# Token rows of a mixture of experts fetched as half rows to all 128 partitions, empty places included

## The chip, the cores and the metric

The kernel runs on 1 core of one Trainium2 chip. The time is device microseconds of that core, one launch of the whole kernel. All data are float32.

## The reference, cut to what matters

The kernel computes a hybrid encoder block of 512 tokens by 2048 features: a token mixer (gated DeltaNet heads and sliding-window attention), a layer norm, then a mixture of 32 experts in which every token goes to 2 of them, and a last layer norm. The change lies in the mixture:

```
glog = xt @ w_route_group                       # 4 groups, the best one is taken
elog = xt @ w_route_expert                      # 8 experts in it, the best two are taken
eid, weights = ...                              # 512 tokens x 2
for each expert e (w_gate, w_up: 2048 x 512, w_down: 512 x 2048):
    rows = the tokens that chose e              # 1024 / 32 = 32 in the mean
    hdn = silu(xt[rows] @ w_gate[e]) * (xt[rows] @ w_up[e])
    y[rows] += weight * (hdn @ w_down[e])
out = layer_norm(ALPHA * xt + y)
```

An expert has 12.58 MB of weights, all of them 402.7 MB, and each is read once.

## The kernel before, in words

Up to about 940 us the kernel computes the mixer, with all 512 tokens on the chip. Then come the first norm and the router, and from about 980 us to the end one block of work for each of the 32 experts, in a fixed order ORD, one after another.

The normed rows (not yet with the bias of the norm) are stored to `h1_scr` in HBM, 512 rows of 8 KB. Each expert has 64 places (SLOTS). The router works out on VectorE and TensorE which token lies in which place: `slot_oh` (L1649) says for each token and choice which place it has in its expert, and `slot_table` (L2214) multiplies this by the token's number, less 512, so that column e of a bank holds, on partition s, the token in place s of expert e, and 0 where the place is empty. `idx_tok` (L1665) is that plus 512: a token, or 512 for an empty place. Places are filled from 0 on.

`gather(t)` (L710) is an indirect DMA that GpSimd issues on its own queue: 64 partitions, one row of 8 KB for each. The index 512 of an empty place is beyond the bound, and nothing is fetched for it; the tile was set to zero once, so it holds an old row or zero. The tile `xb` has two halves by partition: an even expert goes to partitions 0 to 63, an odd one to 64 to 127. A gather waits until the rows before it in that half are turned.

`rows_in(t)` (L2256) turns the rows on TensorE, 16 transposes of 64 x 128 into 128 x 64 (L2250), so that the features lie on the partitions; it runs for expert t+1 in the block of expert t, behind the gate and up matmuls. `rows_out` (L1717) adds the bias on VectorE and writes `xbT`. The block (`block_pe`) then has 64 gate and up matmuls (L2274), the turning of the hidden tile (L2267), 32 down matmuls (L2283), and the combination: 16 matmuls (L2243) spread the last expert's 64 rows to the 512 tokens by a one-hot matrix `place`, and VectorE adds each to `r1` (L1706).

The weights come in 12 pieces of 1 MB per expert: 4 of gate, 4 of up, 4 of down, each to all 128 partitions with one run of 8 KB per partition. SyncE issues them in one stream (L637) into a ring of 15 slots (12 from piece 300 on), each as soon as the piece that lay in its slot has been used. Features are dealt to partitions as "(p k)": partition p has features 16p to 16p+15 and a piece takes 4 of them.

The last two experts in the order (ROWS) are no longer combined into the 512 tokens: their rows are summed, normed and stored by themselves. Their residual rows are fetched by one-hot matmuls (`rows_of`, L2295), the 2048 columns lie as two halves of 64 partitions side by side in `rr_row`, the last step (L1840) writes 64 x 512 pieces back to `xb`, four for each expert, and an indirect DMA (L753) stores the 64 rows to `out`.

A second path for experts with over 64 rows (`leftover_...`) is entered only where there are such; it changes along.

Of the kernel before, what the change touches and what calls it, by code (L numbers as in the profile page):

```python
# [30 lines left out]
P = 128  # L31
# [52 lines left out]


def shape_constants():
# [24 lines left out]
    r = np.zeros((P, 3 * E + TT + S), np.float32)  # L111
# [4 lines left out]
    r[:, 3 * E + TT:] = np.arange(S)[None, :]  # L116
    return k, a, r


def build(nc, x, ln0_g, ln0_b, w_in, conv_w, a_log, dt_bias, gdn_norm_w, sinks, w_o, ln1_g, ln1_b,  # L120
# [6 lines left out]
    gate_v = w_gate[0].rearrange("e (p k) f -> p e k f", p=P)  # L127
    up_v = w_up[0].rearrange("e (p k) f -> p e k f", p=P)
# [3 lines left out]
    with ctx:  # L132
# [10 lines left out]
        h1_scr_v = h1_scr.rearrange("(t p) d -> p t d", p=P)  # L143

# [108 lines left out]
        rc = keep("rc", [P, 3 * E + TT])  # L253
# [27 lines left out]
        idx = keep("idx", [P, 2], I32)  # L281
        idx_tok = at("idx_tok", GD + 47 * KB, [P, E], I32)
# [43 lines left out]
        unused = at("unused", MX, [P, 2 * E * CAP // P], I32)  # L326
        ident = cst[:, K_ID:K_ID + P]
# [112 lines left out]
        RT_IDX = RT_W + 3  # L440
# [10 lines left out]
        ROW_DVE = 13  # L451
# [3 lines left out]
        LF_START, LF_TW, LF_ROWS, LF_HID, LF_HI, LF_SPLIT, LF_DVE = 1, 2, 3, 4, 5, 6, 5 + 4 * TT  # L455
# [61 lines left out]

        def lgT_bank(t):
            return [B0, B2][t % 2]
# [12 lines left out]
        def _(sp):  # L532
# [11 lines left out]
            sp.dma_start(rc[:, :], route_consts[:, 0:3 * E + TT]).then_inc(ld_small, 16)  # L544
# [54 lines left out]
            sp.dma_start(tokens[:, :], route_consts[:, 3 * E + TT:]).then_inc(ld_ln1, 16)  # L599
            sp.dma_start(bT[:, :], ln1_b[0].rearrange("(k p) -> p k", p=P), allow_slow_non_contiguous=True).then_inc(ld_ln1, 16)  # L600
            sp.dma_start(b_rows[:, :], ln1_b[0].rearrange("(p k) -> p k", p=P)).then_inc(ld_ln1, 16)
# [4 lines left out]
            def weight_source(e, i):  # L606

                if i < 8:
                    src = [gate_v, up_v][i % 2][:, bass.ds(e, 1), 4 * (i // 2):4 * (i // 2) + 4, :]
                    return src.rearrange("p o k f -> p (o k f)")  # L610
# [40 lines left out]
        def _(pool):  # L651
# [75 lines left out]
            with pool.If(left > 0):  # L727
# [7 lines left out]
                with pool.Fori(0, left) as i:  # L735
                    row = pool.value_load(ovi[0:1, bass.ds(i + LEFTOVER, 1)], min_val=0, max_val=E * CAP - SLOTS)
                    pool.wait_ge(lf_dve, LF_DVE * i + LF_START)
                    for h in range(2):
                        pool.dma_start(idx[SLOTS * h:SLOTS * (h + 1), :], slot_rows[bass.ds(row, SLOTS), :]).then_inc(lf_rows, 16)
                    pool.reg_mov(r_idx, 48 * i + 32)  # L740
                    pool.wait_ge(h1_stored, 16 * TT)
                    pool.wait_ge(lf_rows, r_idx)
                    pool.indirect_dma_start(xb[0:SLOTS, :], None, h1_scr,
                                            bass.IndirectOffsetOnAxis(ap=idx[0:SLOTS, 0:1], axis=0),
                                            bounds_check=S - 1, oob_is_err=False).then_inc(lf_rows, 16)
# [5 lines left out]
            for m in range(LAST):  # L751
                pool.wait_ge(row_dve, ROW_DVE * (m + 1))
                pool.indirect_dma_start(out[0], bass.IndirectOffsetOnAxis(ap=idx_tok[0:SLOTS, ROWS[m]:ROWS[m] + 1], axis=0),  # L753
                                        xb[SLOTS * m:SLOTS * (m + 1), :], None,
                                        bounds_check=S - 1, oob_is_err=False).then_inc(row_stored, 16)
# [3 lines left out]
        def _(act):  # L759
# [319 lines left out]
            def block_act(t):  # L1079
# [16 lines left out]
                for q in range(4):  # L1096
                    j, h = divmod(q, 2)
# [5 lines left out]
            def leftover_act(i):  # L1103
                act.wait_ge(lf_pe, LF_PE * i + LF_XT)
                for g in range(2):
                    a = act.activation(xbT[1][:, 8 * g:8 * g + 8, :], [R0, R1][g][:, :].rearrange("p (k n) -> p k n", k=8), ACT.Copy)
# [7 lines left out]
                for q in range(4):  # L1114
                    j, h = divmod(q, 2)
# [32 lines left out]
            for h in range(2):  # L1148
                rows = slice(SLOTS * h, SLOTS * (h + 1))
                for to, of in ((g2h, g2), (b2h, b2)):  # L1150
                    act.activation(to[rows, :, :], of[rows, :].rearrange("p (j h c) -> p h j c", j=2, h=2)[:, h, :, :],
# [7 lines left out]
        def _(dve):  # L1159
# [469 lines left out]
            for t in range(TT):  # L1629
# [9 lines left out]
            step(dve.tensor_scalar(pos[:, :, 0], rc[:, 3 * E:3 * E + TT], float(-S), None, ALU.add))  # L1639
# [9 lines left out]
            step(dve.tensor_tensor(slot_oh[:, :, :], tokens[:, 0:SLOTS].rearrange("p (o s) -> p o s", o=1).broadcast_to([P, 2 * TT, SLOTS]),  # L1649
                                   pairs(pos[:, :, :], SLOTS), ALU.is_equal))  # L1650
# [14 lines left out]
            step(dve.tensor_scalar(idx_tok[:, :], B2[:, 0:E], float(S), None, ALU.add))  # L1665
            step(dve.tensor_scalar(tok_all[:, :], B2[:, 0:E], float(S), None, ALU.add))
# [7 lines left out]
                                 rc[:, 3 * E:].rearrange("p (t o) -> p t o", o=1).broadcast_to([P, TT, 2])))  # L1674
# [39 lines left out]
            def row_bias(g):  # L1714
                return b_rows[:, 8 * g:8 * g + 8].rearrange("p (k o) -> p k o", o=1).broadcast_to([P, 8, SLOTS])

            def rows_out(t):  # L1717

                for g in range(2):
                    dve.wait_ge(xT_ps, 2 * t + g + 1)  # L1720
                    dve.tensor_tensor(xbT[t % 2][:, 8 * g:8 * g + 8, :], [R0, R1][g][:, :].rearrange("p (k n) -> p k n", k=8),
                                      row_bias(g), ALU.add).then_inc(xT_d, 1)

            def block_dve(t):
# [17 lines left out]
                if t == HOT - 1:  # L1742
                    for m in range(LAST):
                        rows = slice(SLOTS * m, SLOTS * (m + 1))
                        dve.tensor_scalar(one_hot[rows, :], tokens[rows, :], tok_all[rows, ROWS[m]:ROWS[m] + 1], None,
# [7 lines left out]
            def leftover_dve(i):  # L1753
                dve.wait_ge(lf_rows, 48 * i + 48)
                dve.tensor_copy(slot_tw[:, 0:1], idx[:, 0:1])
                dve.tensor_copy(slot_tw[:, 1:2], idx[:, 1:2].bitcast(F32)).then_inc(lf_dve, 1)
                dve.wait_ge(lf_dve, LF_DVE * i + LF_TW)
                dve.tensor_scalar(place[0][:, :], tokens[:, :], slot_tw[:, 0:1], None, ALU.is_equal)
                dve.wait_ge(lf_act, LF_ACT * i + LF_XBT)
                for g in range(2):  # L1760
                    v = xbT[1][:, 8 * g:8 * g + 8, :]
# [60 lines left out]
            def row_norm(m):  # L1822
# [41 lines left out]
        def _(pe):  # L1864
# [381 lines left out]
            def xT(rows, s_):  # L2246

                for g in range(2):
# [3 lines left out]
                    yield i  # L2252

            xbv = xb[:, :].rearrange("s (p k) -> s k p", k=KD)

            def rows_in(t):  # L2256
# [4 lines left out]
                for i in xT(xbv[SLOTS * s_:SLOTS * (s_ + 1), :, :], s_):  # L2261
# [16 lines left out]
            def down(c, w):  # L2278

                for j in range(2):  # L2280
                    for h in range(2):
                        n0 = (2 * j + h) * F
# [4 lines left out]
            def last_down(c, w):  # L2287
                for q in range(4):
                    j, h = divmod(q, 2)
                    i = mm(DN[j][SLOTS * h:SLOTS * (h + 1), :], hidT[:, c, :], w[:, q * F:(q + 1) * F],  # L2290
                           start=c == 0, stop=c == KF - 1)
                    if c == KF - 1:
                        i.then_inc(w_used, 1)

            def rows_of(m, j, t):  # L2295
# [3 lines left out]
                pe.wait_ge(comb_done, 4 * TT * (t - 1) + (8 if j == 0 else 16))  # L2299
                for tt in range(TT):  # L2300
                    for h in range(2):
                        i = mm(R1[SLOTS * h:SLOTS * (h + 1), :], slot_hot[:, tt, SLOTS * m:SLOTS * (m + 1)],
                               r1[:, tt, (2 * j + h) * F:(2 * j + h + 1) * F], start=tt == 0, stop=tt == TT - 1)
# [55 lines left out]
            def leftover_pe(i):  # L2359
                pe.wait_ge(lf_rows, 48 * i + 48)  # L2360
                for k in range(KD):
                    a = mm([R0, R1][k // 8][:, (k % 8) * SLOTS:(k % 8 + 1) * SLOTS], xbv[0:SLOTS, k, :],
                           cst[0:SLOTS, 0:SLOTS], start=True, stop=True)
# [53 lines left out]
```

## Time and profile before

| | us |
|---|---|
| median of 3 runs | 2006.78 (2005.09 to 2007.88) |
| the profiled execution's own time | 2011.87 |
| its span, first to last instruction | 2010.3 |
| TensorE busy | 1864.9 (93%) |
| VectorE busy | 1031.2 (51%) |
| ScalarE busy | 632.4 (31%) |
| GpSimd busy | 356.6 (18%) |
| mean granted TensorE clock | 0.972 |

The span is a few us shorter than the time of the execution. In the page's 40 slices the share of the 16 DMA engines is 2 to 4 tenths in most slices up to about 900 us and 9 tenths or more in every slice from about 1000 us to 1960 us, where they move some 400 GB/s. A high busy share of an engine says that it had something to do, not that the end waited for it: the chain of waits and the rows of waiting say that.

### The profile page before, as it was taken

To read this page: it belongs to the slowest core of one execution; us is meant where nothing else is said; L and a number is where in the kernel's file an instruction comes from. 1 tells how busy PE (TensorE), PEld (TensorE's weight loads), DVE (VectorE), ACT (ScalarE), POOL (GpSimd) and SP (SyncE) were. 2 spreads that over 40 slices of the span, in tenths; PEclk is the share of its full clock that TensorE was granted. 3 is DMA by queue.
4 is the path that set the end of the run, shared out by engine and by line. 5 is a ranking of instruction groups with operands and counts; after the bars stand their busy time and mean duration, and the time that the engine had idled before them with its cause. 6 is when DMAs were issued, how large, how long until landed. Compare 5 with 4: busy or idle time off the path is not lost.

```text
span 2010.3 us, 25805 instructions
## 1 busy us (share of the span) xinstructions
PE 1864.9 (93%) x10588; PEld 1132.9 (56%) x10588; DVE 1031.2 (51%) x1732; ACT 632.4 (31%) x1040; POOL 356.6 (18%) x292
## 2 busy tenths in 40 slices
PE   5999999999999998999799898998989898988996
PEld 4777887788778777888433333433333333333332
DVE  6456665666533554334655444535444454544356
ACT  6323332243234554113233223231322323132323
POOL 0343333343234322542100000000000000000000
PEclk9999999999999999999799999999999999999998
DMA  7223212222223214438699999999999999999995
GB/s 258 77 64 85 64 51 68 73 64 63 64 72 84 64 53 178 137 105 307 239 400 397 396 405 393 414 398 403 404 400 413 402 413 404 407 402 409 405 400 223
DMA packets 171014, 505.48 MB, mean 251 GB/s; under 512 B 18480, under 2 KB 108720, under 8 KB 117328
## 3 DMA queue, kind: packets, MB, share of 16 engines
q1 hardware_dynamic: 167552, 490.56, 64.3%
q0 software_dynamic: 2768, 9.05, 1.7%
q10 hardware_dynamic: 576, 4.19, 0.5%
q8 instruction: 86, 1.41, 0.3%
q14 instruction: 32, 0.26, 0.0%
HBM read 498.92 MB, written 13.76 MB: 255 GB/s over the span
## 4 chain that ended last, share of the span: by engine, by line
PE 56%; DMA 30%; DVE 9%; ACT 2%; issue 2%; SPq 1%; POOL 0%; DVEq 0%; POOLq 0%; ACTq 0%
DMA ring<-in_w_up 29%; PE bank L2274 10%; PE bank L1869 10%; PE bank L1871 9%; PE bank L1870 9%; PE bank L2283 3%; PE bank L2243 2%; DVE half L1266 1%; PE bank L2016 1%; PE bank L2007 1%; DVE att L1472 1%; DVE sc L1467 1%; PE bank L2025 1%; SPq L637 1%; DVE sc L1487 1%
## 5 line engine op out<-in xcount | busy, mean ns | idle before, releaser
L2274 PE MATMUL bank<-ring,xbT 128*64 128x512 f32 x2048 | 488.7, 621 | 76.0 <-DMA ring<-in_w_up 72.6
L667 POOL TENSOR_TENSOR wlo<-raw,whi 128x512 fp32r<-128x512 f32 x232 | 312.3, 1377 | 525.5 <-ACT whi L790 370.5
L1706 DVE TENSOR_TENSOR r<-r,bank 128x512 f32<-128x512 f32 x464 | 287.7, 682 | 219.5 <-PE bank L2243 219.5
L2274 PEld LDWEIGHTS bank<-ring,xbT 128*64 128x64 f32 x2048 | 155.5, 142 | 362.6 <-issue 359.2
L1869 PE MATMUL bank<-hTh,wlo 128*128 128x512 f32 x704 | 299.8, 426 | 1.9 <-DVE hTl L1199 1.2
L1871 PE MATMUL bank<-hTh,whi 128*128 128x512 f32 x704 | 276.4, 393 | 0.0
L1870 PE MATMUL bank<-hTl,whi 128*128 128x512 f32 x704 | 276.4, 393 | 0.0
L2283 PE MATMUL bank<-ring,hidT 128*64 128x512 f32 x992 | 219.5, 595 | 0.5 <-ACT hidT L1084 0.5
L1711 DVE TENSOR_TENSOR yhl<-yw,yhl 64x512 fp32r<-64x512 f32 x120 | 82.7, 690 | 227.8 <-ACT yhl L1101 224.9
L714 POOL DMA_INDIRECT xb<-h_scr,idx_tok x32 | 31.3, 978 | 899.3 <-PE bank L2250 878.6
L790 ACT ACTIVATE whi<-raw 128x2048 fp32r<-128x2048 f32 x50 | 95.6, 1913 | 199.0 <-PE bank L1871 199.0
L1099 ACT ACTIVATE yw<-bank,wts_all 64x512 f32<-64x512 f32 x120 | 81.6, 680 | 226.7 <-PE bank L2283 224.4
L1869 PEld LDWEIGHTS bank<-hTh,wlo 128*128 128x128 f32 x704 | 132.8, 189 | 32.1 <-issue 3.3
L1871 PEld LDWEIGHTS bank<-hTh,whi 128*128 128x128 f32 x704 | 132.4, 188 | 29.9
L1082 ACT ACTIVATE hid<-bank 64x512 f32<-64x512 f32 x32 | 18.8, 588 | 410.0 <-PE bank L2274 410.0
L2283 PEld LDWEIGHTS bank<-ring,hidT 128*64 128x64 f32 x992 | 69.5, 137 | 135.7 <-issue 135.1
L1870 PEld LDWEIGHTS bank<-hTl,whi 128*128 128x128 f32 x704 | 133.2, 189 | 19.3 <-issue 0.2
L2243 PE MATMUL bank<-yhl,place 128*128 128x512 f32 x480 | 143.8, 421 | 0.0
L2243 PEld LDWEIGHTS bank<-yhl,place 128*128 128x128 f32 x480 | 80.8, 188 | 86.6 <-issue 73.9
L1869 PE MATMUL bank<-whi,mxl 128*128 128x512 f32 x256 | 99.7, 389 | 0.7 <-ACT mixT L969 0.7
L1871 PE MATMUL bank<-whi,mxh 128*128 128x512 f32 x256 | 99.6, 389 | 0.0
L1870 PE MATMUL bank<-wlo,mxh 128*128 128x512 f32 x256 | 99.6, 389 | 0.0
(371 smaller groups left out, 2066.9 us busy)
## 6 DMA issues: line engine op xcount, KB each, us to landing
ring<-in_w_gate SPq DMA_DIRECT2D x128, 1024.0 KB, 28.4
ring<-in_w_up SPq DMA_DIRECT2D x128, 1024.0 KB, 29.1
ring<-in_w_down SPq DMA_DIRECT2D x128, 1024.0 KB, 27.8
raw<-in_w_in SPq DMA_DIRECT2D x44, 1024.0 KB, 5.7
raw<-in_w_o SPq DMA_DIRECT2D x16, 1024.0 KB, 5.0
xt<-in_x SPq DMA_DIRECT2D x4, 1024.0 KB, 8.9
h_scr<-xt SPq DMA_DIRECT2D x4, 1024.0 KB, 7.9
r<-h_scr SPq DMA_DIRECT2D x1, 4096.0 KB, 12.5
```

Source lines behind the costliest of these rows:

```text
L667: i = pool.tensor_tensor(wlo[sl][:, part, :], raw[sl][:, :].rearrange("p (k n) -> p k n", k=KD)[:, part, :], whi[sl][:, part, :].bitcast(F ...
L714: pool.indirect_dma_start(xb[half_, :], None, h1_scr, bass.IndirectOffsetOnAxis(ap=idx_tok[0:SLOTS, ORD[t]:ORD[t] + 1], axis=0), bounds_ch ...
L790: act.activation(whi[sl][:, :, :].rearrange("p k n -> p (k n)"), raw[sl][:, :], ACT.Copy).then_inc(strip_hi, 1)
L1099: act.activation(yw[lo_, q, :], rows, ACT.Copy, scale=wts_all[lo_, ORD[t]:ORD[t] + 1])
L1706: dve.tensor_tensor(v, v, comb_bank(q, tt)[:, :], ALU.add).then_inc(comb_done, 1)
L1711: dve.tensor_tensor(yhl[SLOTS:P, q, :], yw[SLOTS:P, q, :], yhl[SLOTS:P, q, :].bitcast(F32), ALU.subtract).then_inc(yw_split, 1)
L1869: mm(bank, lo_, rh, start=first, stop=False)
L1870: mm(bank, hi_, rl, start=False, stop=False)
L1871: return mm(bank, hi_, rh, start=False, stop=final)
L2243: mm(comb_bank(q, tt)[:, :], place[n % 2][:, tt * P:(tt + 1) * P], yhl[:, q, :], start=True, stop=True).then_inc(comb_ps, 1)
L2274: i = mm(GU[SLOTS * h:SLOTS * (h + 1), :], xT_[:, k, :], w[:, kk * F:(kk + 1) * F], start=k == 0, stop=k == KD - 1)
L2283: i = mm(DN[j][SLOTS * h:SLOTS * (h + 1), :], hidT[:, c, :], w[:, n0:n0 + F], start=c == 0, stop=c == KF - 1)
```

## The change

Everything goes by half rows. `h1_scr` and `out` are seen as 1024 half rows of 4 KB, half row 2n+h being half h of token n. The partition q of a gather fetches half q // 64 of the token in place q % 64, so one gather fills 128 partitions x 1024 columns, and `xb` has its two buffers side by side in the columns. Index of a filled place: 2 x token + half. Index of an empty place: q itself, so that partition q fetches half row q of the scratch; nothing is beyond the bound any more.

The places are dealt to the partitions in another order (place b*8+a to partition a*8+b, in both halves). The features are dealt as "(h p k)": each half has its own 8 per partition, for the weights of gate and up, the bias and the turned rows. Turning takes 8 transposes of 128 x 128 instead of 16. The column quarters that go to each down bank are swapped so that a bank holds column quarters j and j+2. The rows of the last two experts need no moving back: two 128 x 512 steps instead of four of 64 x 512, and their store is one of half rows, where empty places are beyond the bound and skipped, as before. One small VectorE operation is added in the router ahead of the first gather, and one for each of the last two experts.

```diff
-    gate_v = w_gate[0].rearrange("e (p k) f -> p e k f", p=P)
+    gate_v = w_gate[0].rearrange("e (h p k) f -> p e h k f", h=2, p=P)
+    r[:, R_HALF:R_HALF + 1] = i // SLOTS
+    r[:, R_OWN:R_OWN + 1] = i
+    r[:, R_TO_OWN:R_TO_OWN + 1] = 2 * S + i // SLOTS - i
+        h1_halves = h1_scr.rearrange("s (h d) -> (s h) d", h=2)
+        out_halves = out[0].rearrange("s (h d) -> (s h) d", h=2)
+        xb_half = [xb[:, i * D // 2:(i + 1) * D // 2] for i in range(2)]
...
             def gather(t):
-                half_ = slice(SLOTS * (t % 2), SLOTS * (t % 2 + 1))
                 if t >= 2:
                     pool.wait_ge(xT_ps, 2 * (t - 1))
-                pool.indirect_dma_start(xb[half_, :], None, h1_scr,
-                                        bass.IndirectOffsetOnAxis(ap=idx_tok[0:SLOTS, ORD[t]:ORD[t] + 1], axis=0),
-                                        bounds_check=S - 1, oob_is_err=False).then_inc(gathered[t % 2], 16)
+                pool.indirect_dma_start(xb_half[t % 2], None, h1_halves,
+                                        bass.IndirectOffsetOnAxis(ap=idx_tok[:, ORD[t]:ORD[t] + 1], axis=0),
+                                        bounds_check=2 * S - 1, oob_is_err=False).then_inc(gathered[t % 2], 16)
...
-            step(dve.tensor_tensor(slot_oh[:, :, :], tokens[:, 0:SLOTS].rearrange("p (o s) -> p o s", o=1).broadcast_to([P, 2 * TT, SLOTS]),
-                                   pairs(pos[:, :, :], SLOTS), ALU.is_equal))
+            step(dve.tensor_tensor(slot_oh[:, :, :].rearrange("p j (a b) -> p j a b", a=8),
+                                   tokens[:, 0:SLOTS].rearrange("p (o b a) -> p o a b", o=1, b=8).broadcast_to([P, 2 * TT, 8, 8]),
+                                   ...
-            step(dve.tensor_scalar(idx_tok[:, :], B2[:, 0:E], float(S), None, ALU.add))
-            step(dve.tensor_scalar(tok_all[:, :], B2[:, 0:E], float(S), None, ALU.add))
+            step(dve.tensor_scalar(tok_all[:, :], B2[:, 0:E], 0.0, rc[:, R_TO_OWN:R_TO_OWN + 1], ALU.is_lt, ALU.mult))
+            step(dve.scalar_tensor_tensor(out=idx_tok[:, :], in0=tok_all[:, :], scalar=rc[:, R_OWN:R_OWN + 1], in1=B2[:, 0:E],
+                                          op0=ALU.add, op1=ALU.add))
+            step(dve.tensor_scalar(tok_all[:, :], B2[:, 0:E], 0.5, float(S), ALU.mult, ALU.add))
...
                 for j in range(2):
-                    for h in range(2):
-                        rows = slice(SLOTS * h, SLOTS * (h + 1))
-                        dve.scalar_tensor_tensor(out=xb[SLOTS * m:SLOTS * (m + 1), (2 * j + h) * F:(2 * j + h + 1) * F],
-                                                 in0=rr_row[m][j][rows, :], scalar=nm_r[rows, m, 3:4], in1=b2h[rows, j, :],
-                                                 op0=ALU.mult, op1=ALU.add).then_inc(row_dve, 1)
+                    dve.scalar_tensor_tensor(out=xb_half[m][:, j * F:(j + 1) * F], in0=rr_row[m][j][:, :], scalar=nm_r[:, m, 3:4],
+                                             in1=b2h[:, j, :], op0=ALU.mult, op1=ALU.add).then_inc(row_dve, 1)
...
             for m in range(LAST):
                 pool.wait_ge(row_dve, ROW_DVE * (m + 1))
-                pool.indirect_dma_start(out[0], bass.IndirectOffsetOnAxis(ap=idx_tok[0:SLOTS, ROWS[m]:ROWS[m] + 1], axis=0),
-                                        xb[SLOTS * m:SLOTS * (m + 1), :], None,
+                pool.indirect_dma_start(out_halves, bass.IndirectOffsetOnAxis(ap=idx_last[:, m:m + 1], axis=0),
+                                        xb_half[m], None,
...
                 for g in range(2):
-                    for k in range(8):
-                        i = pe.transpose([R0, R1][g][:, k * SLOTS:(k + 1) * SLOTS], rows[:, 8 * g + k, :],
-                                         cst[SLOTS * s_:SLOTS * (s_ + 1), K_ID + SLOTS * s_:K_ID + SLOTS * (s_ + 1)])
+                    for k in range(4):
+                        i = pe.transpose([R0, R1][g][:, k * P:(k + 1) * P], xbv[s_][:, 4 * g + k, :], ident)
```

## Rows read from the trace of the kernel before

**Rows 1.** The page's DMA queues: packets, MB, share of 16 engines.
```profile
q1 hardware_dynamic: 167552, 490.56, 64.3%
q0 software_dynamic: 2768, 9.05, 1.7%
```
**Rows 2.** Busy time of the engines by stretch: PE, PEld, DVE, ACT, POOL, PEclk, DMA share, GB/s.
```profile
1112.60:1890.50 777.90, 702.99 (x3205) 288.34 (x3204) 361.21 (x584) 211.10 (x339) 22.15 (x24) 0.97 1.01 404
```
**Rows 3.** What PE waited for, 1100 to 1940 us: total, times, longest.
```profile
PE bank L2274 <- DMA ring<-in_w_up: 72.6, 60, 4.6
```
**Rows 4.** The chain of waits, 1700 to 1910 us: start, us, what.
```profile
1800.66 31.48 DMA ring<-in_w_up
1832.13 0.14 issue
1832.27 6.47 PE bank L2274 x16
...
1887.86 1.90 PE bank L2250 x16
```
**Rows 5.** GpSimd in order of time: gathers of experts 4, 5, 7 and 31.
```profile
1029.47 0.92 POOL L714 DMA_INDIRECT xb<-h_scr,idx_tok  x1 [26.36 <-PE bank L2250]
1057.07 0.92 POOL L714 DMA_INDIRECT xb<-h_scr,idx_tok  x1 [26.68 <-PE bank L2250]
...
1112.62 0.92 POOL L714 DMA_INDIRECT xb<-h_scr,idx_tok  x1 [26.72 <-PE bank L2250]
...
1890.53 0.92 POOL L714 DMA_INDIRECT xb<-h_scr,idx_tok  x1 [34.07 <-PE bank L2250]
```
**Rows 6.** The DMA view, 1320 to 1340 us, a stretch without a gather.
```profile
DMA packets 1156, 8.42 MB, mean 421 GB/s; under 512 B 129, under 2 KB 129, under 8 KB 129
```
**Rows 7.** The DMA view by queue, 1112.6 to 1890.5 us, 24 gathers.
```profile
q1 hardware_dynamic: 42225, 307.51, 98.1%
q0 software_dynamic: 1920, 6.41, 3.0%
```
**Rows 8.** The same, 14 us from the gather of expert 14, 1340.0 to 1354.0 us.
```profile
q1 hardware_dynamic: 720, 5.24, 93.9%
q0 software_dynamic: 80, 0.29, 7.2%
```
**Rows 9.** The same for expert 15, 1369.8 to 1383.8 us.
```profile
q1 hardware_dynamic: 636, 4.63, 90.8%
q0 software_dynamic: 80, 0.39, 10.5%
```
**Rows 10.** The same for expert 23, 1625.9 to 1639.9 us.
```profile
q1 hardware_dynamic: 735, 5.36, 99.1%
q0 software_dynamic: 80, 0.08, 2.4%
```
**Rows 11.** DMA issues: KB each, median us to landing.
```profile
ring<-in_w_gate SPq DMA_DIRECT2D x128, 1024.0 KB, 28.4
ring<-in_w_down SPq DMA_DIRECT2D x128, 1024.0 KB, 27.8
raw<-in_w_in SPq DMA_DIRECT2D x44, 1024.0 KB, 5.7
raw<-in_w_o SPq DMA_DIRECT2D x16, 1024.0 KB, 5.0
out<-r SPq DMA_DIRECT2D x4, 1024.0 KB, 4.8
```
**Rows 12.** Groups by form, 940 to 2011 us: busy us, mean ns, idle before.
```profile
L2190 PE MATMUL bank<-cst,r 128*128 128x128 f32 x64 | 7.8, 275 | 0.0
L1831 DVE SCALAR_TENSOR_TENSOR rr_row<-rr_row,nm_r,g2h 128x512 f32<-128x512 f32 x4 | 2.8, 747 | 0.2
L1665 DVE TENSOR_SCALAR idx_tok<-bank 128x32 int32<-128x32 f32 x1 | 0.2, 192 | 0.2 <-PE bank L2218 0.2
```
**Rows 13.** All engines in order of time, the first transposes and the end.
```profile
949.65 1.97 PE L2190 MATMUL bank<-cst,r 128*128 128x128 f32 x16
...
1956.01 0.69 DVE L1734 TENSOR_TENSOR hid<-hid,bank 64x512 f32<-64x512 f32 x1 [1.68 <-ACT hid L1082]
...
2001.46 3.09 DVE L1840 SCALAR_TENSOR_TENSOR xb<-rr_row,nm_r,b2h 64x512 f32<-64x512 f32 x4
2005.36 0.92 POOL L753 DMA_INDIRECT out<-xb,idx_tok  x1 [12.26 <-DVE xb L1840]
```

More of the change, by code:

```diff
@@ L83 @@
 J_END = J_SLOPE + QH
+R_HALF = 3 * E + TT
+R_ROW = R_HALF + 1
+R_OWN = R_ROW + 1
+R_TO_OWN = R_OWN + 1
+R_END = R_TO_OWN + 1
 def shape_constants():
@@ L281, in build @@
         idx = keep("idx", [P, 2], I32)
+        idx_half = keep("idx_half", [P, 1], I32)
+        idx_last = keep("idx_last", [P, LAST], I32)
         idx_tok = at("idx_tok", GD + 47 * KB, [P, E], I32)
@@ L516, in ps64, with turned_rows, by_halves @@
             return b[rows, 0:TT * H].rearrange("p (c i) -> p c i", c=TT)
+        def turned_rows(b):
+            return b[:, :].rearrange("p (k h n) -> p k h n", k=4, h=2)
+        def by_halves(tile, g):
+            return tile[:, :, :].rearrange("p (h k) n -> p k h n", h=2)[:, 4 * g:4 * g + 4, :, :]
         def lgT_bank(t):
@@ L598, in _ @@
             sp.dma_start(b1[:, :], ln1_b[0].partition_broadcast(P)).then_inc(ld_ln1, 16)
[L599 removed]
+            sp.dma_start(tokens[:, :], route_consts[:, R_END:]).then_inc(ld_ln1, 16)
             sp.dma_start(bT[:, :], ln1_b[0].rearrange("(k p) -> p k", p=P), allow_slow_non_contiguous=True).then_inc(ld_ln1, 16)
[L601 removed]
+            sp.dma_start(b_rows[:, :].rearrange("p (h k) -> p h k", h=2), ln1_b[0].rearrange("(h p k) -> p h k", h=2, p=P)).then_inc(ld_ln1, 16)
             sp.dma_start(wr[:, :, 0:GROUPS], w_route_group[0].rearrange("(k p) n -> p k n", p=P)).then_inc(ld_ln1, 16)
@@ L1105, in leftover_act @@
                 for g in range(2):
-                    a = act.activation(xbT[1][:, 8 * g:8 * g + 8, :], [R0, R1][g][:, :].rearrange("p (k n) -> p k n", k=8), ACT.Copy)
+                    for h in range(2):
+                        a = act.activation(by_halves(xbT[1], g)[:, :, h, :], turned_rows([R0, R1][g])[:, :, h, :], ACT.Copy)
                 a.then_inc(lf_act, 1)
@@ L1150, in _ @@
                 for to, of in ((g2h, g2), (b2h, b2)):
-                    act.activation(to[rows, :, :], of[rows, :].rearrange("p (j h c) -> p h j c", j=2, h=2)[:, h, :, :],
+                    act.activation(to[rows, :, :], of[rows, :].rearrange("p (h j c) -> p h j c", j=2, h=2)[:, h, :, :],
                                    ACT.Copy).then_inc(rows_act, 1)
@@ L1638, in _ @@
                                    top[:, :, 0:1].rearrange("p t o -> p (t o)"), ALU.subtract))
-            step(dve.tensor_scalar(pos[:, :, 0], rc[:, 3 * E:3 * E + TT], float(-S), None, ALU.add))
+            step(dve.tensor_scalar(pos[:, :, 0], rc[:, 3 * E:3 * E + TT], float(-S), 2.0, ALU.add, ALU.mult))
             assert k_[0] == RT_M
@@ L1720, in rows_out @@
                     dve.wait_ge(xT_ps, 2 * t + g + 1)
-                    dve.tensor_tensor(xbT[t % 2][:, 8 * g:8 * g + 8, :], [R0, R1][g][:, :].rearrange("p (k n) -> p k n", k=8),
-                                      row_bias(g), ALU.add).then_inc(xT_d, 1)
+                    dve.tensor_tensor(by_halves(xbT[t % 2], g), turned_rows([R0, R1][g]), row_bias(g), ALU.add).then_inc(xT_d, 1)
             def block_dve(t):
@@ L1744, in block_dve @@
                         rows = slice(SLOTS * m, SLOTS * (m + 1))
+                        dve.tensor_scalar(idx_last[:, m:m + 1], tok_all[:, ROWS[m]:ROWS[m] + 1], 2.0, rc[:, R_HALF:R_HALF + 1],
+                                          ALU.mult, ALU.add)
                         dve.tensor_scalar(one_hot[rows, :], tokens[rows, :], tok_all[rows, ROWS[m]:ROWS[m] + 1], None,
@@ L1760, in leftover_dve @@
                 for g in range(2):
-                    v = xbT[1][:, 8 * g:8 * g + 8, :]
+                    v = by_halves(xbT[1], g)
                     a = dve.tensor_tensor(v, v, row_bias(g), ALU.add)
@@ L2244, in combine @@
                        start=True, stop=True).then_inc(comb_ps, 1)
-            def xT(rows, s_):
-                for g in range(2):
-                    for k in range(8):
-                        i = pe.transpose([R0, R1][g][:, k * SLOTS:(k + 1) * SLOTS], rows[:, 8 * g + k, :],
-                                         cst[SLOTS * s_:SLOTS * (s_ + 1), K_ID + SLOTS * s_:K_ID + SLOTS * (s_ + 1)])
-                    yield i
-            xbv = xb[:, :].rearrange("s (p k) -> s k p", k=KD)
+            xbv = [xb_half[i].rearrange("s (p k) -> s k p", k=KD // 2) for i in range(2)]
             def rows_in(t):
@@ L2260, in rows_in @@
                     pe.wait_ge(comb_done, 16 * (t - 2) + 10)
-                for i in xT(xbv[SLOTS * s_:SLOTS * (s_ + 1), :, :], s_):
+                for g in range(2):
+                    for k in range(4):
+                        i = pe.transpose([R0, R1][g][:, k * P:(k + 1) * P], xbv[s_][:, 4 * g + k, :], ident)
                     i.then_inc(xT_ps, 1)
@@ L2287, in last_down @@
             def last_down(c, w):
[L2288 to L2293, printed above, removed]
+                for j in range(2):
+                    for h in range(2):
+                        n0 = (2 * h + j) * F
+                        i = mm(DN[j][SLOTS * h:SLOTS * (h + 1), :], hidT[:, c, :], w[:, n0:n0 + F],
+                               start=c == 0, stop=c == KF - 1)
+                        if c == KF - 1:
+                            i.then_inc(w_used, 1)
             def rows_of(m, j, t):
@@ L2360, in leftover_pe @@
                 pe.wait_ge(lf_rows, 48 * i + 48)
-                for k in range(KD):
-                    a = mm([R0, R1][k // 8][:, (k % 8) * SLOTS:(k % 8 + 1) * SLOTS], xbv[0:SLOTS, k, :],
-                           cst[0:SLOTS, 0:SLOTS], start=True, stop=True)
+                for k in range(KD // 2):
+                    a = mm([R0, R1][k // 4][:, (k % 4) * P:(k % 4 + 1) * P], xbv[0][:, k, :], ident, start=True, stop=True)
                 a.then_inc(lf_pe, 1)
```

54 lines of the change are left out of this document (30 added, 24 removed).

## The prediction

> **What bounds the kernel now.** I read the page's slices, then the stretch of the expert blocks, then who waits for whom, then the chain, and last the DMA view stretch by stretch. TensorE is the busiest engine of the page, but in the blocks it is busy 703 of 778 us, while the DMA engines stand at 1.01 of their time and move 404 GB/s [rows 2]. Between 1100 and 1940 us TensorE waits 60 times, 72.6 us in all, and all of it is for weights [rows 3]. So the weight stream sets the pace there. The first blocks, which still live on pieces that were loaded ahead, take 27.6 us each (1057.07 less 1029.47); the 24 from expert 7 to 31 take (1890.53 - 1112.62) / 24 = 32.4 us [rows 5]. The chain says until when: its last piece of waiting for weights ends at 1832 us, and from there it runs through TensorE and VectorE to the end [rows 4]. What shortens the weight stream before 1832 us comes out of the total; what shortens TensorE counts only after.
>
> The stream has a rate of its own: 421 GB/s where no gather runs [rows 6]. Over the 24 gathers that would be 777.9 x 0.421 = 327.5 MB on the weights' queue q1, and it moved 307.5 [rows 7]. So a gather with what comes along displaces (327.5 - 307.5) / 24 = 0.83 MB of weights, though it fetches only 6.41 / 24 = 0.27 MB. Instruction fetches and the like are a few hundredths of that, so I take 0.81 MB, or 0.81 / 0.421 = 1.93 us of the stream for each gather. By its bytes it would be 0.63 us. The excess is what the change can win or lose.
>
> **How one gather's price comes about.** 14 us at 421 GB/s are 5.89 MB. Expert 23 fetches 0.08 MB, some 10 rows, and displaces 5.89 - 5.36 = 0.53 MB [rows 10]. Expert 14 fetches 0.29 MB, 35 rows, and displaces 0.65 [rows 8]. Expert 15 fetches 0.39 MB, 48 rows, and displaces 1.26 [rows 9]. So the price is not one per byte: it has a floor near 0.5 to 0.65 MB that 10 rows reach as 35 do, and about doubles beyond. I read that as skew. 64 partitions over 16 engines are 4 places each; places are filled from 0 on, so 10 rows already give one engine its full 4, and the stream, in which each piece needs all 16 engines, goes by the slowest. 4 rows x 8 KB on one engine are 32.8 KB; at 421 / 16 = 26.3 GB/s that is 1.25 us, or 0.52 MB of the whole stream, and the cheap gathers show 0.53 and 0.65. Beyond 32 places a second set of engines writes too, and the price goes to twice that, as if two engines shared one way into the same partitions.
>
> The Trainium skill has a rule for such a sharing ("SBUF — State Buffer", section "Door 1: The DMA port swizzle"): partition p and p+32 lie on the same DMA port, and 64 partitions reach only half of the ports. By it a gather with over 32 rows puts up to 8 rows on one port, 2.5 us or 1.05 MB, and one with fewer puts 4, 1.25 us; the rows above for experts 14, 15 and 23 agree roughly. By it alone the new gather would cost 1.25 us always.
>
> **The change part by part.**
>
> *The gathers.* Now every engine gets 8 half rows of 4 KB, 32.8 KB, whatever the number of tokens. Bytes go from 0.27 to 0.52 MB a gather, while the largest load of one engine stays at 32.8 KB. The rows go to all 128 partitions as the weights do, so the doubling beyond 32 rows goes. What no row shows is the price c of one 4 KB packet of this queue in an engine's time; a gather costs 8c. Below: at the stream's rate 4.1 KB / 26.3 GB/s = 0.156 us, a gather 1.25 us. Above: an 8 KB row on the slowest engine now costs at most 0.65 / 0.421 / 4 = 0.39 us [rows 8]; if a packet has that price whatever its size, a gather costs 3.1 us. Packet size matters little in this trace: 1 MB in runs of 512 B lands in 5.7 us (w_in), in runs of 2 KB in 5.0 (w_o), in runs of 8 KB in 4.8 (out) [rows 11]. So I take a value near the lower end, half of 0.39 and a little: c = 0.20 us, 1.6 us a gather. Against 1.93 us that is 0.33 us won. The gathers that count are those in the full stream: from expert 2 on, and up to the last that the chain still waits behind, some 26 (experts 2 to 27; the last wait for weights comes earlier when the stream is faster). 26 x 0.33 = 8.6 us off. The break-even is c = 1.93 / 8 = 0.24 us. The ends are 26 x (1.25 - 1.93) = -17.7 us and 26 x (3.1 - 1.93) = +30 us.
>
> *The weights' new order.* A piece still has runs of 8 KB per partition, but they lie 16 KB apart instead of 32 KB. Gate has 32 KB now and down has 8 KB, and they land in 28.4 and 27.8 us [rows 11], so a distance between 8 and 32 KB makes no difference that is clear. I take 0. If all of 28.4 against 27.8 came from the distance, half the way back would gain some 1% of the stream, and at the other end I leave a loss as large, 1% or 8 us; that lies inside the range.
>
> *Turning the rows.* 16 transposes take 1.90 us on the chain [rows 4]. The form with 128 partitions is in the trace at 1.97 us for 16 [rows 13] and 275 ns each, as pipelined [rows 12]; 8 take 0.99 us, so 0.9 us of TensorE per block goes. Up to 1832 us the weights hide that: worth nothing. After it, four or so such places are on TensorE; but the next step waits for ScalarE's and VectorE's hidden tile, 1.3 us behind the gate and up matmuls (0.60 and 0.69 us), so at most 1.90 - 1.3 = 0.6 us is won, and none where the chain goes by VectorE's xbT and sums. I take 0.8 us in all; between 0 and 2.4. If TensorE's cover were gone everywhere it would be worth more, never less. VectorE's writing of xbT in the new order has as many elements; 0.
>
> *The router.* One more VectorE operation of 0.19 us, with its gap 0.21 us [rows 12], ahead of the first gather and of everything that VectorE does behind it, which is on the path to the first block: +0.2 us. slot_oh has as many elements in another order; 0, at most doubled, +0.7 us. The first gather is no later than that: its rows are turned well ahead of the last router step.
>
> *The end.* Of the last expert's four 64 x 512 steps, 3.09 us [rows 13], two of 128 x 512 remain; the form is at 747 ns each [rows 12], so 1.5 us goes, all of it on the chain. The store behind has 128 half rows, skips the empty ones and has no more bytes. It can land up to half a us sooner if the rows are spread better, and GpSimd's issue (0.92 us) could grow with 128 indices: I take -0.2, between -0.6 and +1. The two small operations for idx_last run in the blocks that wait for weights: 0. Extra constants and smaller pieces of the bias land long before their use: 0.
>
> Sum: -8.6 - 0.8 + 0.2 - 1.5 - 0.2 = -10.9 us. On the profiled execution, 2011.87 us, that is 2001.0; its time lies 5.1 us over the median of the runs, so from the median it is 2006.8 - 10.9 = 1996.
>
> **The rivals.**
>
> *The dips stay and the bytes are added (slower).* The excess is then no skew but the price of mixing two queues of any load: a gather keeps its 1.93 - 0.63 = 1.30 us and pays for 0.52 MB instead of 0.27, 1.24 us: 2.54 us. 27 x 0.61 = +16.5 us, less 2.5 for the end and TensorE: 2021 us. It decides from c = 0.24 us on. For it: the stream is full all the time, so 8.2 MB more must go somewhere; packets of both queues are slow in the dip. Against it: 0.08 MB and 0.29 MB have nearly the same price, 0.39 MB twice that, which no fixed excess gives. The Trainium skill's page "DMA: Bandwidth & Descriptors" (section on the anatomy of a DMA) has a DMA cost a constant plus its bytes, which speaks for this rival; by that formula 0.26 MB more at 436 GB/s are an estimated 0.6 us a gather, 16 us in all.
>
> *No net change in the stream.* The fine packets and the doubled bytes eat just what the spreading gives, c between 0.22 and 0.26. Then the end and TensorE remain: 2004 us, 2000 to 2009. For it: the break-even lies in the middle of the range that the rows leave.
>
> *Wholly by the slowest engine (faster still).* c = 0.156: 26 x 0.68 = 17.7 us, and 2.3 beside: 1987 us. This is the far end of the forecast rather than another mechanism.
>
> *TensorE becomes the bound.* Its blocks need 27.6 us against 32.4 now and 32.1 forecast [rows 5], so only the blocks with extra row work near the end come to it, which the count of 26 already holds. No chance of its own.
>
> **How the numbers follow.** Forecast, with its far end, 0.66: 1985 to 2001, centre 1996. No net change 0.15. Bytes added 0.19: 2009 to 2025, centre 2021. Under 0.2%, 4 us, a measurement of this kernel can't tell from no change. Faster by over that (below 2002.8): 0.66 and a little of the second, 0.68. Within: 0.12. Slower: 0.20. The range must reach into the slower case until 1 in 10 is left above: 1985 to 2015. The likeliest case's own is 1987 to 2001.
>
> **What would show it.** Right: in the 14 us behind a gather the weights' queue moves about 5.2 MB whatever the expert, with 0.52 MB on q0; the even pace replaces the 4.6 to 5.4 of now; blocks take 32.1 us; q0's bytes of the whole rise by about 8 MB from 9.05 [rows 1], q1's stay; the mean of the DMA stage rises towards 410 GB/s; the last VectorE steps are two of 0.75 us. Wrong: q1 at 4.8 MB behind every gather (bytes added), or dips as deep for few tokens as for many but longer than 1.6 us; a rate below 421 GB/s between the gathers would convict the weights' new order; a chain in which a wait for xb stands would convict the gather's landing.

## The result, and the profile after

| | before | changed |
|---|---|---|
| median of the runs, us | 2006.35 (4 runs) | 1987.19 (1981.77 to 1990.13, 4 runs) |
| profiled execution's own time | 2011.87 | 1989.5 |
| its span | 2010.3 | 1987.9 |
| TensorE busy | 1864.9 | 1843.3 (93%) |

The ratio is 0.9893, with a 95% interval of 0.9877 to 0.9909: 1.1% or 21 us faster; the two medians lie 19.2 us apart. The forecast was 1996 us, 10.9 us faster. The direction and the place were right, the size was half of what came.

What TensorE waited for between 1100 and 1940 us in the changed kernel (total, times, longest), beside [rows 3]:

```profile
PE bank L2295 <- DMA ring<-in_w_up: 62.3, 67, 4.1
PE bank L2288 <- DVE hid L1761: 8.7, 27, 0.3
```

Its chain of waits around the last wait for weights, beside [rows 4] (start, us, what):

```profile
1755.53 26.89 DMA ring<-in_w_up
1782.41 0.14 issue
1782.55 0.04 PE bank L2295
1782.59 30.92 DMA ring<-in_w_up
1813.51 0.14 issue
1813.64 5.33 PE bank L2295 x16
```

The kernel still lives on the weight stream, now until 1813.5 us instead of 1832.1: 18.6 us of the 22.4 are gained ahead of this point. In the profiled execution the mixer ended 3.1 us later than in that of before (the clearing of `xb` starts at 962.16 against 959.08 us). I take that for scatter: in the profiles of the other kernels below, all with the same mixer, it starts anywhere from 957.0 to 961.7 us. Counted from there, the stream gained 21.7 us.

The DMA view of the changed kernel over the gathers of experts 7 to 29, 1114.59 to 1797.98 us (GB/s in 40 slices; then by queue packets, MB, share of 16 engines):

```profile
GB/s 421 419 422 420 421 420 422 420 421 421 420 421 418 423 419 421 420 421 421 421 421 419 421 420 421 421 422 420 421 420 421 422 420 421 419 421 421 421 421 421
q1 hardware_dynamic: 37828, 275.46, 96.9%
q0 software_dynamic: 3168, 11.54, 4.2%
```

The same for the kernel before, its own experts 7 to 29, 1112.62 to 1816.89 us:

```profile
GB/s 375 422 395 382 416 382 422 378 422 400 420 375 422 402 395 397 397 421 395 421 391 422 393 420 398 391 419 398 421 397 420 405 414 396 388 421 377 420 404 419
q1 hardware_dynamic: 38157, 277.91, 98.0%
q0 software_dynamic: 1760, 6.02, 3.2%
```

This is the finding in two rows. Before, 23 of the 40 slices lie between 375 and 405 GB/s; after, none is below 418, though the gathers move twice the bytes (11.54 MB against 6.02). What a gather displaces, by the working of the prediction over these 22: before 704.27 x 0.421 - 277.91 = 18.6 MB, 0.84 MB each or 2.0 us; after 683.39 x 0.421 - 275.46 = 12.2 MB, 0.56 MB each or 1.3 us. It moves 0.52 MB, so almost nothing is left beside its bytes. The blocks take 31.06 us ((1797.98 - 1114.59) / 22) against 32.01. Over experts 7 to 31, the stretch that the forecast used, they take (1871.26 - 1114.59) / 24 = 31.5 us, against 32.1 forecast and 32.4 before.

The 14 us behind the gather of expert 15 in the changed kernel, 1359.46 to 1373.46 us, beside [rows 9]:

```profile
q1 hardware_dynamic: 732, 5.34, 91.9%
q0 software_dynamic: 144, 0.52, 9.4%
```

The dearest gather of before displaced 1.26 MB, this one 5.89 - 5.34 = 0.55. The same view gives the time of one half row in an engine: 9.4% of 16 engines x 14 us are 21.1 us, over 128 half rows 0.165 us each (the other 16 packets of q0 are small).

The end of the changed kernel (VectorE's last step, now two of 128 x 512, and the store), beside [rows 13]:

```profile
1980.71 1.42 DVE L1868 SCALAR_TENSOR_TENSOR xb<-rr_row,nm_r,b2h 128x512 f32<-128x512 f32 x2
1982.93 1.00 POOL L775 DMA_INDIRECT out<-xb,idx_last  x1 [9.65 <-DVE xb L1868]
```

### The profile page after: what moved, and what is told of

Its sections match the earlier page's. It is cut to its first block, busy times and chain, and to the rows that moved or that the text cites. A ratio compares the mean times of both kernels' runs of the same rounds, so it can differ in the third digit from the quotient of the medians.

```text
span 1987.9 us, 25292 instructions
## 1 busy us (share of the span) xinstructions
PE 1843.3 (93%) x10332; PEld 1113.7 (56%) x10332; DVE 1028.5 (52%) x1731; ACT 632.7 (32%) x1040; POOL 358.9 (18%) x292
## 3 DMA queue, kind: packets, MB, share of 16 engines
q8 instruction: 84, 1.38, 0.3%
## 4 chain that ended last, share of the span: by engine, by line
PE 54%; DMA 32%; DVE 9%; ACT 2%; issue 2%; POOL 0%; SPq 0%; POOLq 0%; DVEq 0%; ACTq 0%
DMA ring<-in_w_up 32%; PE bank L1896 10%; PE bank L2295 9%; PE bank L1897 9%; PE bank L1898 9%; PE bank L2304 3%; PE bank L2270 2%; DVE half L1289 2%; PE bank L2043 1%; PE bank L2034 1%; DVE att L1495 1%; DVE sc L1490 1%; PE bank L2052 1%; DVE sc L1510 1%; PE bank L2324 1%
## 5 line engine op out<-in xcount | busy, mean ns | idle before, releaser
L2295 PE MATMUL bank<-ring,xbT 128*64 128x512 f32 x2048 | 479.7, 611 | 65.3 <-DMA ring<-in_w_up 62.3
```

Of the source, the lines that this page charges most:

```text
L2295: i = mm(GU[SLOTS * h:SLOTS * (h + 1), :], xT_[:, k, :], w[:, kk * F:(kk + 1) * F], start=k == 0, stop=k == KD - 1)
```

## The experiments

Each ratio is to the kernel before on the same chip, in brackets its 95% interval.

**What is undone first: the fetching of empty places**, in three orders of the places. All three keep the half rows and the 128 partitions.

```diff
+            step(dve.tensor_scalar(idx_tok[:, :], B2[:, 0:E], rc[:, R_ROW:R_ROW + 1], None, ALU.add))   # empty: 2 * S + half
```

> The changed kernel with one thing undone: an empty place has an index beyond the bound again and fetches nothing. Places lie as in the change (place b*8+a on partition a*8+b). Bytes of a gather fall from 0.52 to 0.27 MB. Bytes theory (a gather over 128 partitions costs what it moves, in any order): 0.63 us a gather instead of 1.27, 27 gathers, 17 us off the changed kernel's 1987: 1970, 0.982 of before. Slowest-engine theory with an engine for 8 neighbouring partitions: each engine has 4 filled of 8, also 1970. Slowest-engine theory with an engine for partitions p to p+3 and p+32 to p+35 (p a multiple of 4): the filled places of an expert with 32 rows all lie on every other engine, 8 half rows each, so the price stays 1.25 us: 1987, 0.990. Skipping theory (the skipped places themselves made the dips before): the dips come back, 1.9 us a gather: 2004, 0.999.

Measured: 1984.3 us, 0.9892 [0.9876, 0.9909].

The natural order of the places, `tokens[:, 0:SLOTS]` again in `slot_oh`:

> The changed kernel with empty places skipped and the places in their natural order, place s on partitions s and s+64. Bytes theory: 1970, 0.982. Engine for 8 neighbouring partitions: 32 rows fill 8 half rows on half of the engines, 1.25 us as now: 1987, 0.990. Engine for p to p+3 and p+32 to p+35: up to 32 rows give 4 half rows to each engine, 0.62 us, and more than 32 give 8 to some, 1.25 us; about half of the experts each: 0.94 us in the mean, 9 us off: 1978, 0.986. Skipping theory: 2004.

Measured: 1974.2 us, 0.985 [0.983, 0.9871].

The places spread, from a table of constants:

```diff
+    r[:, R_SLOT:R_SLOT + SLOTS] = (8 * (4 * (q // 32) + q % 4) + q % 32 // 4)[None, :]
```

> The changed kernel with empty places skipped and place s put on partition 32*(s//32) + 4*(s%8) + (s//8)%4 of each half, so that consecutive places go to different groups of partitions. Engine for p to p+3 and p+32 to p+35: n rows give each engine n/8 half rows rounded up, 4.2 in the mean, 0.65 us: 27 x 0.62 = 17 us off the changed kernel: 1970, 0.982, the best of the three. Engine for 8 neighbouring partitions: 32 rows fill partitions 0 to 31 of each half, 1.25 us: 1987. Bytes theory: 1970. Skipping theory: 2004.

Measured: 1968.9 us, 0.9818 [0.9802, 0.9835]. The same bytes in three orders give three times, so bytes are not all (the intervals of the second and the third just touch; a later run of the third gave 0.9816 again). Skipping as such costs nothing, which fells that theory. The order of the three, and their sizes, are those of the slowest engine with an engine for partitions p to p+3 and p+32 to p+35 (expected 1987, 1978, 1970). The Trainium skill ("DMA: Bandwidth & Descriptors", section "The descriptor swizzle") states this assignment for a transfer to 128 partitions; the three times agree with it, and the rival with 8 neighbouring partitions would have put the first at 1970 and the third at 1987.

The traces of the first and the third over experts 7 to 29 (1113.71 to 1793.80 us, and 1113.34 to 1781.65 us) say how the slowest engine acts:

```profile
GB/s 419 419 424 418 423 418 421 422 420 420 420 422 420 421 419 422 419 421 420 422 420 419 414 419 417 415 410 420 418 414 422 419 416 403 417 416 410 392 423 421
DMA packets 41324, 284.11 MB, mean 418 GB/s; under 512 B 5934, under 2 KB 5934, under 8 KB 7402
q1 hardware_dynamic: 38125, 277.65, 98.6%
```
```profile
DMA packets 40887, 280.93 MB, mean 420 GB/s; under 512 B 5886, under 2 KB 5886, under 8 KB 7354
q1 hardware_dynamic: 37688, 274.47, 98.8%
```

With places on every other engine the 22 blocks take 680.1 us, spread 668.3 us, and yet the rates are 418 and 420 GB/s, which explains 3 us of the 12. In the slower one 3.2 MB more had arrived in the stretch for the same 22 blocks. I read that as the lightly loaded engines running ahead into pieces that are not complete; that was not measured engine by engine. The slices fit it: up to the middle they stand at 418 to 424 GB/s, gathers or not, and later some fall, to 392 at the lowest. One such fall is at 1747 to 1749 us, 15 us behind the gather of expert 27, when that gather has long landed: 324 GB/s. So uneven load makes no dip at its gather. It adds up over the experts and comes out later.

**Whole rows, nothing skipped.** The kernel before, with an index of its own for each empty place:

```diff
+    r[:, R_OWN:R_OWN + 1] = i % SLOTS
+    r[:, R_TO_OWN:R_TO_OWN + 1] = S - i % SLOTS
...
```

> The kernel before with one thing changed: an empty place fetches a whole row of its own (row number = place), so 64 rows of 8 KB go to 64 partitions every time, 0.52 MB, as many bytes as in the change. Theory of the shared way into the partitions (64 partitions are reached by half of the ways): 8 rows on each way, 65.5 KB, 2.5 us a gather against 1.93 before: 27 x 0.57 = 15 us slower, 2021, 1.008. Slowest engine alone, no shared way: 4 rows on each of 16 engines, 1.25 us, 18 us faster: 1988, 0.991. Skipping theory: the dips go with the skipping, 1988 too. Bytes on top of a fixed excess: 2.54 us, 2022.

Measured: 2042.5 us, 1.0188 [1.0168, 1.0209]. 14 us behind the gather of expert 15, 1381.7 to 1395.7 us:

```profile
GB/s 398 398 421 445 421 375 421 492 398 398 421 445 398 187 187 211 211 281 234 187 234 281 234 304 234 304 421 421 421 421 445 398 375 445 445 445 398 445 445 375
q1 hardware_dynamic: 620, 4.51, 85.7%
q0 software_dynamic: 80, 0.52, 15.3%
```

The direction is that of the shared way, and just as well that of bytes on top of a fixed excess (2022); this run can't tell them apart. The size is over both: 5.89 - 4.51 = 1.38 MB or 3.3 us, where 2.5 were expected by both and 1.3 is what the same bytes cost in the change. For 4.5 us (13 slices of 0.35) the two queues together run at little over half of their rate, so the weights alone at less than that. So neither the number of bytes (the change moves as many) nor the skipping makes the dip, but something about whole rows to 64 partitions: the size of the row, or the 64.

**Half rows in two gathers of 64 partitions.**

```diff
-                pool.indirect_dma_start(xb_half[t % 2], None, h1_halves, ... idx_tok[:, ...]
+                for h, ix in enumerate((idx_tok, idx_hi)):
+                    pool.indirect_dma_start(xb_half[t % 2][SLOTS * h:SLOTS * (h + 1), :], None, h1_halves, ... ix[0:SLOTS, ...]
```

> The changed kernel with one thing changed: each gather is issued as two, the first half rows to partitions 0 to 63, then the second to 64 to 127. The same 128 half rows of 4 KB, the same bytes, the same place order, nothing skipped. Two small operations of VectorE more in the router (+0.4 us). Shared-way theory (64 partitions are reached by half of the ways, all 16 engines crowd on them): the dips come back, at the price that whole rows to 64 partitions with nothing skipped had for the same bytes, 3.1 us against 1.3: 27 x 1.8 = 48 us slower than the changed kernel, 2035, 1.014 of before. By bytes and the load of each engine alone: nothing changes but a second issue: 1988, 0.990.

Measured: 2039.5 us, 1.0165 [1.0141, 1.0189]. 14 us behind the gathers of expert 15, 1377.67 to 1391.67 us:

```profile
GB/s 398 515 445 375 375 421 421 421 398 445 468 351 410 246 257 304 199 351 199 316 293 211 363 222 293 269 257 316 258 386 375 445 398 398 445 375 421 421 468 468
q1 hardware_dynamic: 617, 4.51, 88.5%
q0 software_dynamic: 160, 0.52, 13.4%
```

The dip is back with 4 KB rows, so it is not the size of the row. What is left is the 64 partitions of a DMA, or that there are two DMAs for each expert; the whole rows above had a dip with one.

**Two gathers of 128, each filling 64.** Who writes, or where to? The same partitions are filled one half after the other, but by DMAs that span all 128.

```diff
+                    if h:
+                        pool.wait_ge(gathered[t % 2], 32 * (t // 2) + 16)
+                    pool.indirect_dma_start(xb_half[t % 2], None, h1_halves, ... ix[:, ...]     # the other half's indices are beyond the bound
```

> The changed kernel with each gather issued as two over all 128 partitions: the first has its indices for partitions 64 to 127 beyond the bound and fills 0 to 63, the second the reverse, and waits for the first. The same bytes go to the same partitions as in the kernel with two gathers of 64 partitions; what differs is the shape of the DMA and so which engine writes which partition. If the dips come of engines that write to partitions that are another engine's in the weights' DMAs (the deal of 64 rows to 16 engines): no dips, 1.3 us for both, 1989, 0.991. If they come of 64 partitions being reached at a time, whoever writes them: as with two gathers of 64, 2035, 1.016. If the slowest engine sets the price with no leeway (8 engines have 8 half rows, then the other 8): 2 x 1.25 us, 33 us over the changed kernel: 2020, 1.006.

Measured: 1992.2 us, 0.9927 [0.9911, 0.9942]. The 20 us that hold both gathers of expert 16, 1394.4 to 1414.4 us:

```profile
GB/s 475 393 393 475 410 426 393 442 410 377 426 385 434 434 369 451 434 377 475 377 459 410 393 459 377 459 410 426 402 402 418 402 451 410 377 467 442 393 442 377
q1 hardware_dynamic: 1073, 7.82, 94.0%
q0 software_dynamic: 288, 0.52, 7.1%
```

No dip, 47 us less than with gathers of 64, for the same bytes to the same partitions. The dips hang on the DMA's shape. The second gather waits for the first here, which the kernel with gathers of 64 did not do; but the changed kernel sends all 128 half rows at once and has no dip either. The reading that fits is the expected one: in a DMA to 64 partitions some engines write to partitions that belong to others in the weights' DMAs. That is argued and not shown: which engine writes what in such a DMA is seen in no view here.

**Whole rows, places spread over blocks of four.**

```diff
+    r[:, R_SLOT:R_SLOT + SLOTS] = (16 * (q % 4) + q // 4)[None, :]
```

> The kernel before with places put on its 64 partitions in another order, place s on partition 4*(s%16) + s//16, so that 32 rows give two to each block of four partitions; skipping and bytes as before. If a DMA to 64 partitions gives each of 16 engines four neighbouring partitions, and the slowest engine sets the price: 2.2 rows in the mean, 0.7 us instead of 2.0: 35 us faster than before, 1970. If the shared way sets it, 8 ways get n/8 rows each, 4.3 in the mean, 1.35 us: 1988, 0.991. If the price goes with the bytes as in the kernel with whole rows and nothing skipped (1.28 MB for 0.52), 0.67 MB for 0.27, 1.6 us: 1995, 0.994. If it is something else about 64 partitions, no change, 2005.

Measured: 2018.4 us, 1.0056 [1.0038, 1.0075], slower, which no theory had. Expert 15 (0.39 MB, 47 or 48 rows), 1374.9 us on, and expert 23 (10 rows), 1632.31 us on, 14 us each:

```profile
q1 hardware_dynamic: 673, 4.89, 91.6%
...
q1 hardware_dynamic: 769, 5.60, 99.4%
```

Displaced are 1.00 and 0.29 MB, in place of 1.26 and 0.53 [rows 9, 10]: for these two cheaper. Yet over experts 7 to 29 (1114.54 to 1823.90 us) it is 0.92 MB a gather against 0.84, so others got dearer. So the floor that 10 rows had depends on where the rows lie, but spreading them over more of the 64 partitions wins nothing in the mean. Why it costs more is not shown; that more rows then lie in another engine's partitions is a guess.

**The weights' order alone**, on the kernel before:

```diff
-    gate_v = w_gate[0].rearrange("e (p k) f -> p e k f", p=P)
+    gate_v = w_gate[0].rearrange("e (h p k) f -> p e h k f", h=2, p=P)
...
```

> The kernel before with the change's order of the features alone: gate and up weights and the bias dealt as (h p k), the columns of the rows picked to match; whole rows, 64 partitions, 16 transposes, skipping as before. Expected by every theory: 0, 2005 (within 4 us), 421 GB/s between gathers. If runs 16 KB apart instead of 32 KB were read better, part of the change's gain is here: 1 to 1% faster.

Measured: 2006.9 us, 0.9991 [0.998, 1.0002]. Nothing, as forecast.

**What all gathers still cost.** This kernel leaves out the gathers of experts 2 to 31:

```diff
+                if t < 2:
                     pool.indirect_dma_start(xb_half[t % 2], None, h1_halves,
...
```

> The changed kernel without the gathers of experts 2 to 31: their blocks compute on the rows of experts 0 and 1 (the output leaves the others' rows out). This measures what all gathers still cost. 1.27 us x 27 = 34 us off the changed kernel: 1953, 0.974, unless TensorE's own 27.6 us a block, or its longer blocks near the end, come to bound first; the stream alone needs 12.58 / 0.421 = 29.9 us a block, so they should not before the last six.

Measured: 1950.8 us, 0.9719 [0.9701, 0.9736]: 33 to 36 us under the medians of the changed kernel (1984.0 and 1987.2), where 27 gathers at 1.27 us had given 34. The gathers that are left cost their bytes, and leaving them out gives that back.

**One shared half row for all empty places:**

> The changed kernel with one thing changed: every empty place fetches the same half row (half 0 or 1 of token 0) instead of one of its own; 32 reads in the mean of the same 4 KB in each half. By bytes and engines: 1987, 0.990. If reads of one place in HBM wait for each other, and since every engine has 4 of them in the mean: dearer; at twice the time for these packets 27 x 0.6 = 17 us, 2004, 0.999.

Measured: 1982.9 us, 0.9887 [0.9872, 0.9902], against 0.9899 of the changed kernel on the same chip: no difference. A place of its own for each empty one buys nothing.

**The change and the best version side by side:**

> The changed kernel itself, beside the others of this call: 1987, 0.990 of before.

> Empty places skipped and places spread over the groups of partitions, once more and in more rounds, beside the changed kernel on the same chip. By the traces a gather displaces 0.31 MB instead of 0.56: 27 x 0.25 / 0.421 = 16 us faster than the changed kernel: 1970, 0.982 of before.

Measured: 1984.0 us, 0.9899 [0.9884, 0.9915], and 1968.7 us, 0.9816 [0.98, 0.9832]. Skipping with spread places beats both kernels, by 0.8% and 1.8%.

## Why the prediction was right and wrong, step by step

*The bound.* Right: the stream sets the time up to some 20 us before 1832 us, and 21.7 of the gain lie there.

*The price of a gather now.* Forecast 1.93 us, measured with the same working over experts 7 to 29 2.0. Right.

*The price of one half row, c.* This is the term that was mis-sized. I took 0.20 us, above the 0.156 that the stream's rate gives, because the cheap gathers of before cost 0.39 us a row on the slowest engine, which is more than their bytes. Measured is 1.32 / 8 = 0.165 us with all that comes along, and the time of the packets themselves says the same (9.4% of 16 x 14 us over 128). The excess that I carried over was no property of the packet; it was the dip of a DMA to 64 partitions, which the change removes whole. The experiment with the same half rows to 64 partitions has it back. With 0.7 us a gather instead of 0.33, 27 gathers give 18 to 19 us, the rest is the end.

*The reading of the dips.* Only half right. I had one mechanism, the slowest engine, with a shared way beyond 32 rows. The runs show two. The first is the shape of the DMA: one to 64 partitions makes the packets of the weights slow as long as it lasts. The floor of the cheap gathers was that already, as expert 23 shows. Here are 2 us of the kernel before in which half of its ten rows are fetched, 1630.3 to 1632.3 us, and below 2 us without a gather, 1620 to 1622 us (packets, MB, share of 16 engines):

```profile
q1 hardware_dynamic: 55, 0.39, 95.5%
```
```profile
q1 hardware_dynamic: 117, 0.84, 101.6%
```

The engines spend nearly as much of their time on the weights' packets, but move less than half of the bytes: a packet takes about twice as long. By my reading the engines without rows would have gone on at their pace, or stood idle behind the one with four rows. That four rows on one engine come to 0.52 MB and 0.53 were measured is then chance. The rival of mixing two queues had this row for it ("packets of both queues are slow in the dip"); I named it and did not follow it. Nor is there a clear step at 32 rows, as the shared way wants it: expert 18 (0.31 MB, 1466.87 to 1480.87 us) displaces 5.89 - 5.05 = 0.84 MB and expert 10 (0.34 MB, 1208.23 to 1222.23 us) 5.89 - 4.85 = 1.04, between the 0.65 and 1.26 of experts 14 and 15. With 7 of expert 14's 35 rows on one way, 7 / 8 of the 1.05 MB of the prediction, 0.92 MB, were due; its 0.65 does not agree.

The second mechanism is uneven load. Alone it makes no dip at the gather and is paid in the sum over the experts.

*The weights' order.* Forecast 0, measured 0.9991 [0.998, 1.0002].

*Turning, router, end.* From the end of the last wait for weights to the end of the span it was 178.2 us and is 174.4: 3.8 us against 2.5 forecast (0.8 + 1.5 + 0.2). VectorE's last step gives 3.09 - 1.42 = 1.7 of them, where 1.5 was forecast. From its end to the end of the span it was 5.75 us and is 5.77, so the store gained nothing. The remaining 2.1 us, against 0.8 forecast for the turning, come with 32 instructions of TensorE fewer in this stretch (652 against 684, which is four turnings of 8 less each), TensorE busy 150.9 us against 154.7, and a granted clock of 0.92 against 0.90; how they share them was not taken apart. The router's extra operation does not show before the first gather (15.1 us behind the clearing of `xb` in both); the first block starts 0.6 us later, against 0.2 forecast.

*The rivals.* Bytes on top of a fixed excess gave 2021; the excess went, the bytes stayed, and it fell. No net change fell as well. The far end of the forecast, the floor of c, 1987, is what came. I had seen it as an end of the range, with the rows for packet size speaking for it, and chose a middle value out of caution. That the far end hit is in part luck: its price for a half row, the rate of the stream, is close to what was measured, but that the excess of before would go was argued from four rows on one engine, and the rows above say otherwise.

## What to carry to other kernels

A stream that is always full hides where it is slow: look for slices in which the rate falls, and divide what was displaced by what the second DMA moved. Here an indirect DMA to 64 partitions cost three times its bytes in the mean beside a full stream (0.84 MB for 0.27), and half rows to 128 partitions cost little more than their bytes (0.56 for 0.52). Once that is so, fewer bytes pay again: skip the empty places, and deal the filled ones so that every engine gets the same sum. And look at the time of a single packet in the dip: it tells engines that wait from engines that are slow.

## What the runs showed of the hardware that I had not expected

- A gather of 0.52 MB to 64 partitions brings the 16 engines, both queues together, to little over half of their rate for some 4.5 us (rows of 8 KB, 187 to 304 GB/s against 421). Two gathers with half rows of 4 KB bring them to two thirds for some 5.6 us (199 to 363 GB/s). Even ten rows make the weights' packets beside them take twice as long (0.39 MB in 2 us against 0.84, at 95.5% and 101.6% of the engines' time). Two gathers that span 128 partitions and fill 64 of them each time leave the rate at 418 GB/s in the mean.
- 8 half rows of 4 KB on each engine cost 1.3 us, where the same bytes of weights in runs of 8 KB take 1.25 (0.52 MB at 421 GB/s).
- Indices beyond the bound cost no time that shows: with them skipped and the places spread, 22 blocks run at the rate of the stream (420 GB/s).
- 32 reads of the same 4 KB in one gather cost no more than 32 of different ones (0.9887 against 0.9899).
